# Gate columns on four column groups, rotations one place later, returned rows over four banks, output sent by tile

## The reference, cut to what matters

```
for l in range(DEPTH):                                   # 2
    h = rms_norm(x, norm_mix_g[l])
    q, k_c, v_c, k_s, v_s, k_w, v_w, nsa_g, sgu_in, s5_in, branch_g = split(h @ w_in[l])
    nsa_gates = sigmoid(nsa_g)                           # 24 columns of w_in
    q_rot, k_slc, k_win = partial_rope(q / k_s / k_w, positions)
    x = x + merged @ w_mix_o[l]
    h = rms_norm(x, norm_ffn_g[l])
    x = x + sum over the token's 2 experts: weight * (silu(h @ w_gate[e]) * (h @ w_up[e])) @ w_down[e]
return rms_norm(x, norm_final_g)
```

## Time and profile before

| | |
|---|---|
| time, median of 3 runs | 1936.79 us (1935.34 to 1937.72) |
| profiled execution | 1934.61 us, span 1932.8 us |
| PE | busy 1865.5 us, 97% of the span |
| DVE | busy 993.6 us, 51% |
| ACT, POOL | 25%, 7% |
| DMA | 482.13 MB, mean 249 GB/s, some 425 GB/s in the expert stages |
| granted clock of PE | mean 0.986 of full speed |
| chain that ended last | PE 46%, DVE 3%, the rest small |

### The profile page before, as it was taken

How to read it: one execution, slowest core, us unless ns; L and a number is a source line. 1 busy time by engine, 2 the same in 40 slices (tenths; PEclk the granted TensorE clock), 3 DMA queues, 4 the chain that set the end, 5 groups by cost and what they waited for, 6 DMA issues and landing times. The chain is left out here.

```text
span 1932.8 us, 26668 instructions
## 1 busy us (share of the span) xinstructions
PE 1865.5 (97%) x10360; PEld 1170.3 (61%) x10361; DVE 993.6 (51%) x1929; ACT 479.5 (25%) x854; POOL 144.5 (7%) x237
## 2 busy tenths in 40 slices
PE   6999999999999999999899999999999999999995
PEld 4768777778445455454457777777774445455442
DVE  7764655676344343343467555557673344343344
ACT  4403444423111111111234134444321111111112
POOL 3600000050000000000063000000400000000000
PEclk9999999999999999999989999999999999999998
DMA  4222111253999999999712221114359999999993
GB/s 168 66 81 78 66 66 66 89 159 145 378 427 427 424 427 425 427 428 420 310 50 85 76 83 66 66 45 123 125 218 403 427 427 426 425 425 424 426 428 154
DMA packets 59952, 482.13 MB, mean 249 GB/s; under 512 B 9808, under 2 KB 22608, under 8 KB 30672
## 3 DMA queue, kind: packets, MB, share of 16 engines
q1 hardware_dynamic: 59856, 480.80, 61.3%
HBM read 476.59 MB, written 4.19 MB: 249 GB/s over the span
## 5 line engine op out<-in xcount | busy, mean ns | idle before, releaser
L1877 DVE TENSOR_TENSOR x_tokens<-x_tokens,ps 128x512 f32<-128x512 f32 x240 | 161.7, 687 | 236.7 <-PE ps L1041 235.5
L1107 PE MATMUL ps<-arena,branch 128*64 128x512 f32 x512 | 226.6, 595 | 0.0
L1107 PE MATMUL ps<-slabs,branch 128*64 128x512 f32 x512 | 226.6, 595 | 0.0
L1057 PE MATMUL ps<-arena 128*64 128x512 f32 x512 | 225.1, 592 | 0.5 <-DVE arena L1867 0.5
L1057 PE MATMUL ps<-slabs,arena 128*64 128x512 f32 x512 | 225.0, 592 | 0.5 <-issue 0.5
L1058 PE MATMUL ps<-arena 128*64 128x512 f32 x512 | 225.1, 592 | 0.0
L1058 PE MATMUL ps<-slabs,arena 128*64 128x512 f32 x512 | 225.0, 592 | 0.0
L779 PE MATMUL ps<-h_hi,w_parts 128*128 128x512 f32 x768 | 210.8, 408 | 1.5 <-DVE w_parts L1490 1.5
L1057 PEld LDWEIGHTS ps<-slabs,arena 128*64 128x64 f32 x512 | 70.1, 137 | 146.5 <-issue 146.4
L779 PEld LDWEIGHTS ps<-h_hi,w_parts 128*128 128x128 f32 x768 | 135.1, 189 | 38.8 <-issue 9.2
L1057 PEld LDWEIGHTS ps<-arena 128*64 128x64 f32 x512 | 70.0, 137 | 145.9 <-issue 145.9
(11 more groups left out here) (353 smaller groups left out, 3129.2 us busy)
## 6 DMA issues: line engine op xcount, KB each, us to landing
arena<-in_expert_w_gate SPq DMA_DIRECT2D x32, 2048.0 KB, 12.2
slabs<-in_expert_w_gate SPq DMA_DIRECT2D x32, 2048.0 KB, 15.1
slabs<-in_expert_w_up SPq DMA_DIRECT2D x32, 2048.0 KB, 19.6
arena<-in_expert_w_up SPq DMA_DIRECT2D x32, 2048.0 KB, 16.7
arena<-in_expert_w_down SPq DMA_DIRECT2D x32, 2048.0 KB, 9.5
slabs<-in_expert_w_down SPq DMA_DIRECT2D x32, 2048.0 KB, 14.0
slabs<-in_gate_w SPq DMA_DIRECT2D x24, 1024.0 KB, 4.8
slabs<-in_dense SPq DMA_DIRECT2D x22, 1024.0 KB, 5.8
```

Source lines behind the costliest of these rows:

```text
L1057: nc.tensor.matmul(ps[0:64, BANK_GU[b], :], xk, low[:, k, :], start=(k == 0), stop=(k == ND - 1), tile_position=(0, 0))
L1107: done = nc.tensor.matmul(ps[64 * b:64 * b + 64, BANK_Y[half], :], hidT[:, k, CAP * b:CAP * (b + 1)], w_down[b][:, k, half * 512:(half + 1 ...
L1877: v.tensor_tensor(xs, xs, ps[:, BANK_BACK[n % 2], :], ALU.add).then_inc(s["back_added"], 1)
```

## The change

1. First block: the angle work of DVE is cut into pieces, and the scaling of tile 0 comes after five of its ten operations, that of tile 1 after six, tiles 2 and 3 after eight; the last two operations come behind tile 3. ACT squares the next tile before it takes the root of the one ahead. POOL makes a 128x24 matrix `stack` of four identities above each other, and clears 8 columns behind the weights.
2. Gate columns: the weights (32 columns, of which 8 belong to the next chunk or to cleared memory) are now the loaded operand and the 128 tokens of a tile the moving one; chunk k goes to column group k mod 4. ACT copies the four partial sums (128x512) to `nsa_parts`, four matmuls with `stack` behind the two S5 jobs add them up, and ACT's Tanh moves behind its second S5 copy.
3. `rotate(n)` comes at u = n + 2, no longer n + 1.
4. In the last two pairs the returned rows lie in four banks, DVE does both products of the hidden rows before the first sum, and in the last pair four of the eight rows are returned between the halves of the down product.
5. SP sends each output tile inside the layer's block as soon as it is scaled. The repair path for overfull experts sends them again.

```
-                act.wait_ge(g["var"], t + 1)
-                nc.scalar.activation(rstd[:, t:t + 1], sumsq[:, t:t + 1], ACT.Sqrt).then_inc(g["sd"], 1)
+                if t >= 1:
+                    root(t - 1)
+            root(NT - 1)
...
-                reduce_angle(nc, link, ang, kk, rr, r2)
-                scale_tokens(dve, turn_g, False)
+                turns_of(nc, link, ang, kk)
+                link(nc.vector.scalar_tensor_tensor(rr, kk, -PI_1, ang, ALU.mult, ALU.add))
+                scale_token(dve, turn_g, 0, False)
+                link(nc.vector.scalar_tensor_tensor(rr, kk, -PI_2, rr, ALU.mult, ALU.add))
+                scale_token(dve, turn_g, 1, False)
+                link(nc.vector.scalar_tensor_tensor(rr, kk, -PI_3, rr, ALU.mult, ALU.add))
+                link(nc.vector.tensor_scalar(rr, rr, PI_SAFE, -PI_SAFE, ALU.min, ALU.max))
+                scale_token(dve, turn_g, 2, False)
+                scale_token(dve, turn_g, 3, False)
+                quarter_from(nc, link, rr, r2)
...
-                            last = nc.tensor.matmul(ps[:, BANK_S[0], t * 24:(t + 1) * 24], hT[:, k, t * P:(t + 1) * P], wnsa[:, k, :],
-                                                    start=(k == 0), stop=(k == ND - 1))
+                            r = 32 * (k % 4)
+                            last = nc.tensor.matmul(ps[r:r + 32, BANK_S[0], t * P:(t + 1) * P], wnsa[k], hT[:, k, t * P:(t + 1) * P],
+                                                    start=(k < 4), stop=(k >= 4), tile_position=(0, r))
...
+                    def nsa_sums():
+                        pe.wait_ge(s["nsa_parted"], 1)
+                        for t in range(NT):
+                            last = nc.tensor.matmul(ps[:, BANK_S[1], t * 24:(t + 1) * 24], nsa_parts[:, t * P:(t + 1) * P], stack, start=True, stop=True)
...
-                        if 1 <= u <= 6:
-                            rotate(u - 1)
+                        if 2 <= u <= 7:
+                            rotate(u - 2)
...
-                    nc.scalar.activation(nsa_g.rearrange("p t c -> p (t c)"), ps[:, BANK_S[0], 0:NT * 24], ACT.Tanh, scale=0.5).then_inc(s["nsa_read"], 1)
+                    nc.scalar.activation(nsa_parts, ps[:, BANK_S[0], :], ACT.Identity).then_inc(s["nsa_parted"], 1)
...
+                        down_half(i, 0)
+                        if final:
+                            for n in range(4, 8):
+                                back_free(i, n, 4)
+                                row_back(n, banks)
+                        down_half(i, 1)
...
+                        for t in range(NT):
+                            sp.wait_ge(s["next_xn"], t + 1)
+                            sp.dma_start(io["out"][0, t * P:(t + 1) * P, :], x_unit[:, t, :]).then_inc(fin, 16)
```

More of the change, by code:

```diff
@@ L232, in build @@
         small = {k: view(O_SMALL + a, n) for k, (a, n) in SMALL.items()}
-        wnsa = view(O_SMALL + SMALL["wnsa"][0], ND, 24)
+        w0 = SMALL["wnsa"][0]
+        wnsa = [view(O_SMALL + w0 + 24 * k, 32) for k in range(ND)]
+        nsa_end = view(O_BBT, 8)
+        stack = view(O_BBT + 8, 24)
+        nsa_parts = view(O_V, S)
         st = O_STAT
@@ L356, in scaled, with scale_token @@
             return nc.vector.tensor_scalar(x_unit[:, t, :], x[:, t, :], one, None, ALU.mult)
[L358 to L367, removed]
+        def scale_token(dve, g, t, weighted):
+            one = slice(t, t + 1)
+            dve.wait_ge(g["sq"], t + 1)
+            nc.vector.tensor_scalar(sumsq[:, one], sumsq[:, one], 1.0 / D, EPS, ALU.mult, ALU.add).then_inc(g["var"], 1)
+            dve.wait_ge(g["sd"], t + 1)
+            nc.vector.reciprocal(rstd[:, one], rstd[:, one]).then_inc(g["rstd"], 1)
+            dve.wait_ge(g["rstd"], t + 1)
+            scaled(t, weighted).then_inc(g["xn"], 1)
         def turn_tile(t):
@@ L1047, in rows_ready, with back_free, down_half @@
                         pe.wait_ge(s["y_lo_ready"], 2 * i)
-                    def back_free(i, n):
-                        pe.wait_ge(s["back_added"], 8 * i + (n - 9))
+                    def back_free(i, n, ahead):
+                        pe.wait_ge(s["back_added"], 8 * i + (n - 7 - ahead))
+                    def down_half(i, half):
+                        for k in range(NH):
+                            for b in range(2):
+                                done = nc.tensor.matmul(ps[64 * b:64 * b + 64, BANK_Y[half], :], hidT[:, k, CAP * b:CAP * (b + 1)],
+                                                        w_down[b][:, k, half * 512:(half + 1) * 512], start=(k == 0), stop=(k == NH - 1),
+                                                        tile_position=(0, 64 * b))
+                        done.then_inc(s["down_done"], 1)
                     def gate_up(k, b, i, m, at):
@@ L1080, in pair @@
                             pe.wait_ge(s["xe_ready"], 2 * m + 2 + q)
-                        for n in range(8):
+                        banks = BANK_BACK_LAST if last_quad else BANK_BACK
+                        final = last_quad and at == 3
+                        for n in range(4 if final else 8):
                             if not first:
                                 if n >= 2 or not second:
-                                    back_free(i, n)
-                                row_back(n)
+                                    back_free(i, n, 4 if final or last_quad and n >= 2 else 2)
+                                row_back(n, banks)
                             if not last_quad:
@@ L1898, in pair @@
                         hid_of(i, 0)
-                        if not first:
-                            add_back(i, 0, second)
+                        banks = BANK_BACK_LAST if last_quad else BANK_BACK
+                        if not first and not last_quad:
+                            add_back(i, 0, second, banks)
                         hid_of(i, 1)
                         if not first:
-                            for n in range(1, 8):
-                                add_back(i, n, second)
+                            for n in range(0 if last_quad else 1, 8):
+                                add_back(i, n, second, banks)
                         if not last_quad:
@@ L2169, in _ @@
                     def _(sp):
-                        if not last_layer:
+                        if last_layer:
+                            for t in range(NT):
+                                sp.wait_ge(so["turn_xn"], t + 1)
+                                sp.dma_start(io["out"][0, t * P:(t + 1) * P, :], x_unit[:, t, :]).then_inc(fin, 16)
+                            sp.wait_ge(fin, 32 * NT)
+                        else:
                             sp.wait_ge(x_saved, 16 * NT * (layer + 1))
```

53 lines of the change are left out of this document (39 added, 14 removed).

## The result

| | before | changed |
|---|---|---|
| median of the runs (4 each) | 1936.35 us | 1912.37 us (1910.96 to 1913.73) |
| ratio, 95% interval | | 0.9879 (0.9865 to 0.9893) |
| span of the profiled execution | 1932.8 us | 1909.2 us |
| granted clock, mean | 0.986 | 0.990 |

A forecast was written before the change was run, and what follows sets the result against it. PE, busy 97% of the span, was taken as the bound. The terms summed to 33.4 us off the profiled 1934.61, giving 1901.2; the runs' median lies 2.2 above, so 1903.4 us, range 1898 to 1912.

The forecast's parts named there:

- Gate columns: Gate jobs ahead of S5: 0.5 us each instead of 1.70, low clock behind them gone; 4.8 and 7.4 us gained.
- The 0.9 us of idle PE inside the first S5 job: First layer: PE was to wait 0.9 us for DVE's low features, in the third part of that job.
- Rotations: Between `s5_within` and `s5_output`: the wait at the first rotation goes, no other replaces it; 7.2 and 5.7 us gained.
- Rival 4: Slower than before: 32-column matmuls leave PE at 1.2 GHz, some 65 us per layer, in full some 2000; chance 0.02.
- First block: Start of the kernel: DVE's last scaling at about 17.2 and PE's last transposes earlier; 0.6 us gained, bounds 0 and 1.4.
- Last pairs: Last expert pairs: 1.1 us per layer from the last pair, 0.2 in the first layer from the pair before.
- rival 1: The clock falls elsewhere, behind a longer wait for expert 31, or stays low behind the gate jobs; 1906 to 1910, chance 0.17.
- the 2 us become waiting: Pair before the last: the 2 us of waits saved there turn into PE waiting for expert 31's weights.
- Mix stage: Stage where PE waits for POOL's low weights; the forecast held no loss there, 0 in the first layer.
- Rival 3: Gain given back to DVE or POOL (S5's tables, DVE's powers); 1908 to 1916, chance 0.17 together with two other rivals.
- Layer change and output: Layer change: no term, 0. Output at the end: one last DMA instead of four, 5.3 us gained.
- The change of block (1.3 us) runs under it: End of the kernel: the block change was taken to be hidden under the last output DMA.

The follow-up runs named there:

- align205: The changed kernel with PE's code moved by an address directive; 1902.07 us, ratio 0.9832.
- mix_by_piece: The changed kernel with PE's mix-stage products waiting for the low weights piece by piece, not for the whole slab; 1904.84 us, ratio 0.9833.

## Why the prediction missed

**Gate columns: right.** Forecast 0.5 us a job, 4.8 and 7.4; found 0.57 or less, 5.3 and 7.0. The 0.9 us of idle PE inside the first S5 job did not come; DVE's low features were there in time and the jobs were some 0.4 longer in all than forecast, which makes the half microsecond more. The cadence of the nearest row was the right guide. What the term left out is what the lead is worth at the end: by itself the gate part made the kernel 4.8 us faster, half clock elsewhere and the branch took the rest. The rule of the Trainium skill, TensorE: Matmul & The Clock Gate (What overlaps and what doesn't), with the loads of 0.110 us in the earlier trace rows one behind the other, would give 1.76 us a job; the trace disagrees, with 1.01 for two.

**Rotations: right.** 7.2 and 5.7 against 6.8 and 5.3, with no wait left; taking them back cost 9.2 us by the medians.

**Rival 4: did not come, and its sum was off.** No half clock stands between the gate jobs and `s5_output` in either layer. All 65 us per layer at half clock would have added 130, to about 2033 and not some 2000, and a quarter of that stretch, not half, would have cost the 33.

**First block: direction right, too small.** The last scaling started at 16.56 us, not 17.2, and the last 8 transposes took 1.09 us, not 1.65: a transpose took 421 ns in the first two tiles and 273 in the last two. They ended 2.15 us earlier than before, of which 1.4 reached PE's next job.

**Last pairs: the error of rival 1.** For the last pair itself 1.1 per layer was about right (1.0 by the shifts in the first). The sentence "the 2 us become waiting" was right as well: 1.98 and 2.31 us. But I priced this wait at nothing beyond itself, while half clock came behind it in both layers, 1.7 us each. Rival 1 names this very place, and I gave it 0.17.

**Mix stage: a step that is not in the working.** The lead of 13 us was carried through some 300 us of other stages without asking what is late there. The profile of before had the row: PE waited 0.96 us for these weights in the first layer and 1.25 in the second. Rival 3 named POOL, but its tables for S5, and not this. It cost 2.8 us, about half of it the longer wait and half the low clock.

**Layer change and output: the step that failed most, by its size and by its mechanism.** "The change of block (1.3 us) runs under it" took the 1.3 us of before as a property of the block. It hangs on where PE's code lies. The change made PE's code longer, and that cost 2.9 us at the layer change, for which the sum had no term at all, and 2.5 at the end, 5.4 of the missing 9.8. With the code in place the tail is 3.04 us against the 3.3 to 4.3 of my bounds, so that the output part is worth 6.1, not 5.3: the 512 KB landed 2.6 us behind the issue, sooner than either row I took. DMA: Bandwidth & Descriptors of the Trainium skill (Anatomy of one DMA) gives 3.2 us, an estimate by a fit for DMAs of another path; the trace is below it.

The Trainium skill, Runtime: NRT & Kernel Launch (Instruction fetch mechanics), has the rule that I did not weigh: "A taken branch whose target isn't in the current 2-page window forces a DMA fetch of the target page before execution can continue". The traces agree, with 3.4 to 4.1 us in place of 0.34 to 0.46; no run here shows how large that window is.

**Open:** what decides whether a wait of 1.7 us is followed by half clock. The runs of the kernel before range from 1930 to 1940 us on one chip, with a mean clock from 0.989 down to 0.984; at 1.7 us a time, those 10 us are some six falls more or fewer, and it is why single executions with 5 us less or more say little about an edit.

## What to carry to other kernels

A branch over a long path that is never taken can wait for its code, and code added hundreds of microseconds ahead can bring that about: look at the durations of the branch instructions on the busiest engine, and if they are microseconds long, set the place of the code by an address directive, as `align205` does. When a stretch is shortened, walk on through all later stages and ask at each short wait of the bounding engine who must come earlier too. And price each new wait of PE above some 1.7 us with half clock behind it, or fill it.

## What was not expected of the hardware

- A counting instruction that does nothing else takes PE 0.086 us (13.8 us for 160).
- Across the twelve profiled executions, away from the first block and the layer change: none of 11 waits of PE from 1.15 to 1.54 us was followed by half clock, 20 of 32 from 1.67 to 1.86 us were (the half clock began between 0.5 and 2.5 us behind the wait's end), and so were all 15 of 1.98 us and more (in nine of them it began inside the wait). The same wait (router, 1.70 us) went both ways within one kernel and between kernels.
- The time lost to half clock need not all reach the end: PE waits for the weights of expert 31, and what it loses ahead of the experts can shorten that wait. In the second layer it was 1.23 us in `mix_by_piece`, with half clock behind the router, against 2.31 in the changed kernel, with none there. That the one made the other is likely, not shown.
